# A hybrid attention and MLP layer on one core: the single heads' states and scores by token tiles of 128 instead of chunks of 64

## The chip, the cores and the metric

The program runs on one core of one Trainium2 chip. The metric is the device time of one execution in microseconds (us); less is better. Engines are named as the profile names them: PE is TensorE (PEld its weight loads), DVE is VectorE, ACT is ScalarE, POOL is GpSimd, SP is SyncE, which issues most DMAs.

## What is computed

One decoder layer over 1,024 tokens of width 1,024: an input projection, eight heads of gated linear attention (four "GLA" heads with keys 64 wide, computed two at a time as pairs, and four "HGRN2" heads with keys 128 wide, the **single heads**), an output projection and an MLP. The part that the change touches is, per head:

```
def chunk_gated_linear_attention(q, k, v, log_a, chunk):       # chunk = 64
    cum = jnp.cumsum(log_a.reshape(b, h, n, chunk, dk), axis=3)
    q_rel = q * jnp.exp(cum - cum_mid);  k_rel = k * jnp.exp(cum_mid - cum)
    scores = jnp.where(causal, jnp.einsum('bhncd,bhnsd->bhncs', q_rel, k_rel), 0.0)
    o_intra = jnp.einsum('bhncs,bhnse->bhnce', scores, v)
    k_to_end = k * jnp.exp(cum_last - cum)
    chunk_update = jnp.einsum('bhncd,bhnce->bhnde', k_to_end, v)
    # state_n+1 = exp(cum_last) * state_n + chunk_update
    o_inter = jnp.einsum('bhncd,bhnde->bhnce', q * jnp.exp(cum), states_prev)
    return o_intra + o_inter
```

## The kernel before

Everything is fp32. Large products are split into a high and a low fp32r part and made as three products over 128 rows, 128 weight columns and 512 moving columns. The products of the attention are plain fp32; each stands in the trace as **two** instructions (and two weight loads), so "x8" is four products.

The order of the work is written out by hand for every engine. The heads come in groups: P0, P1 (the paired heads), H0 (the first single head), then three times `paired` (groups 3, 4, 5: single heads 1 to 3) and `gates` (group 6). Each group projects its own head's columns and at the same time carries out the attention of the head **before** it. So the four single heads' attention lies in groups 3, 4, 5 and 6; their keys and queries are prepared in H0 (DVE function `group`) and in `paired` 3, 4 and 5.

On PE, `two_pairs` (L2051) is the order within groups 3 to 6: projection pieces P1, P2, P6, P5, P4, P3 of an early pair of column blocks, then P1, P2, P6, P5, P4, P3 of a late pair, and between them the steps of `attention_steps` (L210 to L219). With a head's two halves of 512 tokens the steps are: transposes of the keys k(0); state updates up(0); scores sc(0); k(1) and sc(1), with P4 early after them; outputs o(0); P3 early; ss(0), the sum of squares of the outputs; P1 late; up(1); P2 late; o(1); P6 and P5 late; ss(1); P4 and P3 late.

- `updates` (L1866): per half 8 (then 7) products k_nat^T v_nat, one for each chunk of 64 tokens. A chunk's rows are the lower or the upper 64 partitions, and the products alternate between them. PE waits for ACT's copies k_nat and v_nat.
- `scores` (L1853): per half four 128x128 products k_rel^T q_rel, one per tile of 128 tokens. DVE's `masks` (L2680) copies out what `causal` allows; `causal` is 0 in the block between a tile's two chunks (L946).
- `outputs` (L1884): per half four products of v_nat and the masked scores (L1893), then eight of 128 rows, 128 weight columns and 64 moving columns with the states and the queries q_cum (L1901).
- ss (L1844): ones times sq_hi and sq_lo, 512 columns each. ACT squares the outputs and makes sq_hi (L1358 to L1363); DVE makes sq_lo (`low_squares`, L2701), for which PE waits.

DVE in `paired` (L2724): states(0) (eight operations of 128 columns, each waiting for the last), masks(0), the joins of the projection's pieces, masks(1), the forget gate (L2748), low_squares(0), L2752, a scan (L2755), states(1) (seven operations), the two differences (L2759, L2762), then k_rel, k_end (L2769), a join, the copy `decay` (L2773), q_cum (L2778), q_rel (L2781), a weight sum, low_squares(1), more joins. ACT (L1402) makes the exponentials between them. POOL makes the low parts of the weights (`pair_low`, L973).

In H0 the same is done by `group` (L2455); there ACT waits for q_cum_ready (L1321) before it reads the last unit, and further down its queue come the copy k_nat (L1351) and what PE needs for up(0) of group 3.

## Time and profile before

| what | value |
|---|---|
| median of 3 runs | 1164.52 us (1164.21 to 1164.85) |
| the profiled execution, its own time | 1163.81 us |
| its span in the profile | 1162.1 us |
| granted TensorE clock, mean | 0.995 |
| PE busy | 1135.4 us, 98% of the span |
| DVE busy | 865.3 us, 74% |
| ACT busy | 612.4 us, 53% |
| POOL busy | 494.9 us, 43% |
| matmul instructions | 5555 |

The busy time of an engine counts matmuls whose ends are modelled and overlap, so 98% means that PE hardly ever stood without a matmul in flight. Groups 3 to 6 lie between some 224 and 439 us of the span.

### The profile page before, as it was taken

The numbers are of one execution on the slowest core, as the hardware profiler recorded it, in microseconds if no ns is written. First come the engines' busy times: TensorE is split into PE (matmuls) and PEld (weight loads), VectorE is DVE, ScalarE is ACT, GpSimd is POOL, SyncE is SP. The second block draws the span as 40 slices with busy tenths as digits, with TensorE's granted clock in tenths as the row PEclk, the third lists the DMA queues.
The fourth block names the chain that finished last, engine by engine and source line by source line (L and its number), as shares of the span: only waits on it lengthen the run. The fifth ranks groups of instructions, "written<-read, shape, count | busy, mean of one in ns | idle before, by whom it ended". The sixth has DMA issues, their size and how long they took to land.

```text
span 1162.1 us, 15677 instructions
## 1 busy us (share of the span) xinstructions
PE 1135.4 (98%) x5555; PEld 939.4 (81%) x5555; DVE 865.3 (74%) x1044; ACT 612.4 (53%) x933; POOL 494.9 (43%) x320
## 2 busy tenths in 40 slices
PE   7999999989999999999999999999999999999996
PEld 7788788777878788888888888888888888788886
DVE  6898887587778677377976775677795884966876
ACT  7763555756566566255654555455664433524424
POOL 1021122134243345336534343344566675665751
PEclk9999999999999999999999999999999999999999
DMA  9777387344353546722445344544624637447203
GB/s 356 263 234 272 129 202 209 79 127 134 92 173 100 155 122 213 241 77 82 143 156 184 142 156 125 182 145 159 195 64 161 220 92 264 150 133 278 71 1 145
DMA packets 162949, 186.73 MB, mean 161 GB/s; under 512 B 7604, under 2 KB 119352, under 8 KB 159928
## 3 DMA queue, kind: packets, MB, share of 16 engines
q1 hardware_dynamic: 160472, 179.44, 46.7%
q0 software_dynamic: 2400, 6.29, 2.8%
q8 instruction: 45, 0.74, 0.3%
q14 instruction: 32, 0.26, 0.1%
HBM read 138.51 MB, written 40.89 MB: 154 GB/s over the span
## 4 chain that ended last, share of the span: by engine, by line
PE 92%; DVE 2%; DMA 2%; ACT 2%; SPq 1%; issue 1%; DVEq 0%; ACTq 0%
PE unit_bank L1764 19%; PE unit_bank L2178 9%; PE unit_bank L2180 9%; PE unit_bank L2179 9%; PE small_bank L2178 9%; PE small_bank L2180 9%; PE small_bank L2179 9%; PE small_bank L1764 4%; PE unit_bank L2025 3%; PE unit_bank L2027 3%; PE unit_bank L2026 3%; PE small_bank L1901 2%; DMA ada_slot<-in_w_ada_dram 2%; PE small_bank L1803 1%; PE small_bank L1893 1%
## 5 line engine op out<-in xcount | busy, mean ns | idle before, releaser
L1016 POOL TENSOR_TENSOR wr_lo<-quarter,wr_hi 128x512 fp32r<-128x512 f32 x122 | 197.2, 1628 | 174.6 <-ACT wr_hi L1552 174.4
L2178 PE MATMUL unit_bank<-op_hi,wr_hi 128*128 128x512 f32 x452 | 176.8, 391 | 0.9 <-issue 0.9
L2180 PE MATMUL unit_bank<-op_hi,wr_lo 128*128 128x512 f32 x452 | 176.0, 389 | 0.0
L2179 PE MATMUL unit_bank<-op_lo,wr_hi 128*128 128x512 f32 x452 | 176.0, 389 | 0.0
L2178 PE MATMUL small_bank<-op_hi,wr_hi 128*128 128x512 f32 x448 | 174.6, 390 | 0.0
L2179 PE MATMUL small_bank<-op_lo,wr_hi 128*128 128x512 f32 x448 | 174.4, 389 | 0.0
L2180 PE MATMUL small_bank<-op_hi,wr_lo 128*128 128x512 f32 x448 | 174.4, 389 | 0.0
L1552 ACT ACTIVATE wr_hi<-wr_full 128x512 fp32r<-128x512 f32 x90 | 56.8, 631 | 174.8 <-DVE wr_full L2921 174.8
L2921 DVE TENSOR_TENSOR wr_full<-quarter,quarter 128x512 f32<-128x512 f32 x90 | 89.1, 991 | 56.8 <-PE small_bank L2180 22.9
L1552 ACT ACTIVATE wr_hi<-quarter 128x512 fp32r<-128x512 f32 x136 | 82.9, 626 | 89.3 <-PE unit_bank L2180 49.1
L1764 PE MATMUL unit_bank<-a_hi,w_hi 128*128 128x512 f32 x304 | 121.1, 398 | 0.0
L1764 PE MATMUL unit_bank<-a_lo,w_hi 128*128 128x512 f32 x304 | 118.5, 390 | 0.0
L1764 PE MATMUL unit_bank<-a_hi,w_lo 128*128 128x512 f32 x304 | 118.5, 390 | 0.0
L1016 POOL TENSOR_TENSOR wr_lo<-wr_full,wr_hi 128x512 fp32r<-128x512 f32 x48 | 80.5, 1680 | 77.4 <-ACT wr_hi L1552 48.1
L2178 PEld LDWEIGHTS unit_bank<-op_hi,wr_hi 128*128 128x128 f32 x452 | 84.8, 188 | 19.3 <-issue 2.1
L2180 PEld LDWEIGHTS unit_bank<-op_hi,wr_lo 128*128 128x128 f32 x452 | 84.9, 188 | 17.8
L2179 PEld LDWEIGHTS unit_bank<-op_lo,wr_hi 128*128 128x128 f32 x452 | 84.9, 188 | 17.8 <-issue 0.2
L2180 PEld LDWEIGHTS small_bank<-op_hi,wr_lo 128*128 128x128 f32 x448 | 84.1, 188 | 17.6
L2178 PEld LDWEIGHTS small_bank<-op_hi,wr_hi 128*128 128x128 f32 x448 | 84.2, 188 | 17.4 <-POOL wr_lo L1016 0.2
L2179 PEld LDWEIGHTS small_bank<-op_lo,wr_hi 128*128 128x128 f32 x448 | 84.1, 188 | 17.3
L931 POOL TENSOR_TENSOR w_lo<-raw,w_hi 128x1024 fp32r<-128x1024 f32 x11 | 29.4, 2677 | 123.9 <-ACT w_hi L1073 123.9
L973 POOL TENSOR_TENSOR pw_lo<-pw_full,pw_hi 128x512 fp32r<-128x512 f32 x24 | 36.6, 1527 | 84.2 <-ACT pw_hi L1337 69.3
(370 smaller groups left out, 2382.5 us busy)
## 6 DMA issues: line engine op xcount, KB each, us to landing
quarter<-in_w_mlp_dram SPq DMA_DIRECT2D x128, 256.0 KB, 4.1
hidden_scratch<-hid SPq DMA_DIRECT2D x98, 256.0 KB, 2.3
ada_slot<-in_w_ada_dram SPq DMA_DIRECT2D x48, 512.0 KB, 6.6
op_full<-hidden_scratch SPq DMA_DIRECT2D x21, 1024.0 KB, 4.8
pair_quarter<-in_w_in_dram SPq DMA_DIRECT2D x32, 256.0 KB, 3.6
piece_x<-t_scratch SPq DMA_DIRECT2D x16, 512.0 KB, 4.1
piece_y<-t_scratch SPq DMA_DIRECT2D x32, 256.0 KB, 3.4
raw<-in_w_out_dram SPq DMA_DIRECT2D x16, 512.0 KB, 3.9
```

The lines of the kernel that those rows point to most:

```text
L931: pool.tensor_tensor(w_lo[slot][:, :, :], raw[slot][:, :, :], w_hi[slot][:, :, :].bitcast(F32), ALU.subtract).then_inc(wlo_ready, 1)
L973: pool.tensor_tensor(pw_lo[place][:, :, :], pair_source(prod), pw_hi[place][:, :, :].bitcast(F32), ALU.subtract).then_inc(pair_lo, 1)
L1016: pool.tensor_tensor(wr_lo[slot][:, :, :], split_source(n), wr_hi[slot][:, :, :].bitcast(F32), ALU.subtract).then_inc(wr_lo_pool, 1)
L1552: act.activation(wr_hi[slot][:, :, :], split_source(n), ACT.Copy).then_inc(wr_hi_ready, 1)
L1764: return pe.matmul(out_ap, left, right, start=start, stop=stop)
L2025: pe.matmul(dst, wh, hi[:, k, :], start=k == 0 and prod not in (P6, P3), stop=False, skip_group_check=True)
L2026: pe.matmul(dst, wh, lo[:, k, :], start=False, stop=False, skip_group_check=True)
L2027: mm = pe.matmul(dst, wl, hi[:, k, :], start=False, stop=k == KH - 1, skip_group_check=True)
L2178: pe.matmul(dst, wh, ah, start=opens, stop=False, skip_group_check=True)
L2179: pe.matmul(dst, wh, al, start=False, stop=False, skip_group_check=True)
L2180: mm = pe.matmul(dst, wl, ah, start=False, stop=k == KH - 1, skip_group_check=True)
L2921: dve.tensor_tensor(dst[:, :, :], a[:, :, :], b[:, :, :], op).then_inc(w_sum, 1)
```

## The change

For the single heads the states are carried by tiles of 128 tokens. Eight states per head remain of sixteen; `updates` makes 4 (then 3) products per half over all 128 rows; `outputs` makes 3 (then 4) products of 128 moving columns with the states. For this the keys of a tile's first chunk are scaled by the decay of the second (`far_keys`), the queries of the second chunk by the decay of the first (`tile_queries`), and a tile's decay is the product of both. What a tile's second chunk takes from its first no longer goes through a state: `scores` makes, after each tile's product, one more with 128 rows, 64 weight columns (k_near, the keys of the first chunk) and 64 moving columns (q_near, the queries of the second), into the block of the scores that the mask left out, and DVE sets `causal` to 1 there (in H0). k_near and q_near are two new tiles of 128x512. PE's key transposes wait for far_keys (`k_far_ready`), the scores also for q_cum_ready. In `paired` the multiplication of k_end becomes one into k_near for the first chunks and one in place for the second; in H0 k_near is a copy. The update of the second half uses bank 3 alone. The paired heads' work is as before. The diff, cut to its core (the renamed counts of semaphores and the changed signature of update_chunks are left out):

```diff
@@ -209,12 +209,12 @@
         s[0] += [("k", 0, 0, 0)]
-        s[1] += [("up", 0, 0, 2), ("up", 1, 0, 3)]
+        s[1] += [("up", 0, 0, 2)]
         s[2] += [("sc", 0, 0, 1)]
...
         s[5] += [("ss", 0, 0, 1)]
-        s[6] += [("up", 2, 1, 3), ("up", 3, 1, 0)]
+        s[6] += [("up", 1, 1, 3)]
         s[7] += [("o", 0, 1, 2)]
@@ -248,18 +248,21 @@
     if kind == "up":
-        return (0, 0, 8)[gi] if isinstance(gi, int) and gi < 3 else 16 + 4 * (gi - 3)
+        return (0, 0, 8)[gi] if isinstance(gi, int) and gi < 3 else 16 + 2 * (gi - 3)
     if kind == "chunks":
-        return (0, 0, 30)[gi] if isinstance(gi, int) and gi < 3 else 60 + 15 * (gi - 3)
+        return (0, 0, 30)[gi] if isinstance(gi, int) and gi < 3 else 60 + 7 * (gi - 3)
     return (0, 0, 4)[gi] if isinstance(gi, int) and gi < 3 else 8 + 2 * (gi - 3)
-def update_chunks(prev, q):
-
-
-    per = 2 if prev == "P" else 4
-    first = 2 * per * (q // 2) + q % 2
-    return [n for n in range(first, first + 2 * per, 2) if n < NC - 1]
+def update_chunks(q):
+
+    first = 4 * (q // 2) + q % 2
+    return [n for n in range(first, first + 4, 2) if n < NC - 1]
+
+
+def update_tiles(half):
+
+    return [n for n in range(4 * half, 4 * half + 4) if n < TT - 1]
@@ -384,6 +383,8 @@
         decay = at("decay", 206.6875, [P, NC])
+        decay_tile = at("decay_tile", 206.65625, [P, TT])
+        k_near, q_near = at("k_near", 188.5, [P, TT, CH]), at("q_near", 190.5, [P, TT, CH])
         x_stat = at("x_stat", 206.6875, [P, TT])
@@ -1377,7 +1387,7 @@
                     if p % 2 and p < PAIRS - 1:
-                        act.wait_ge(filled["up"], before("up", FIRST_PAIRED + p // 2) + 4)
+                        act.wait_ge(filled["up"], before("up", FIRST_PAIRED + p // 2) + 2)
                     act.wait_ge(six_done, six_of(p, P1))
@@ -1832,7 +1842,10 @@
                 elif kind == "k":
-                    pe.wait_ge(k_end_ready, gi)
+                    if gi >= FIRST_PAIRED:
+                        pe.wait_ge(k_far_ready, gi - 1)
+                    else:
+                        pe.wait_ge(k_end_ready, gi)
                     mm = turn([k_end[:, t * P:(t + 1) * P] for t in range(4 * half, 4 * half + 4)], b)
@@ -1855,36 +1868,45 @@
                 pe.wait_ge(q_rel_ready, gi)
+                if prev == "H":
+                    pe.wait_ge(q_cum_ready, gi)
+                    pe.wait_ge(k_far_ready, gi - 1)
                 for i in range(4):
...
                         mm = product(SB[b][:, i * P:(i + 1) * P], k_rel[mine, t], q_rel[mine, t])
+                        if prev == "H":
+                            mm = product(SB[b][0:CH, i * P + CH:(i + 1) * P], k_near[:, 4 * half + i, :], q_near[:, 4 * half + i, :])
                         if i == 3:
...
-                width = 2 if prev == "P" else 1
                 for _, _, half, _, _ in pieces:
...
                     pe.wait_ge(read["v"], before("v", gi) + (half + 1 if prev == "P" else 0))
-                chunks = [update_chunks(prev, which) for _, which, _, _, _ in pieces]
+                if prev == "H":
+                    for _, _, half, b, _ in pieces:
+                        for n in update_tiles(half):
+                            mm = product(SB[b][:, n % 4 * P:(n % 4 + 1) * P], k_nat[:, n % 4, :], v_nat[:, 0, n, :])
+                        mm.then_inc(filled["up"], 1)
+                    return
+                chunks = [update_chunks(which) for _, which, _, _, _ in pieces]
                 for place in range(len(chunks[0])):
...
                             r = slice(CH * (n % 2), CH * (n % 2) + CH)
-                            dst = SB[b][:, place * P * width:(place + 1) * P * width]
-                            mm = product(dst, k_nat[r, (n // 2) % 4, :], v_nat[r, 0:width, n // 2, :])
+                            dst = SB[b][:, place * P * 2:(place + 1) * P * 2]
+                            mm = product(dst, k_nat[r, (n // 2) % 4, :], v_nat[r, 0:2, n // 2, :])
                             if place == len(mine) - 1:
...
-                width = 2 if prev == "P" else 1
                 for _, which, half, b, _ in pieces:
@@ -1892,8 +1914,17 @@
                                   masked[:, slot, i * P:(i + 1) * P], start=i == 0, stop=False, skip_group_check=True)
-                pe.wait_ge(read["up"], before("chunks", gi) + (8 * pieces[0][2] + 7) * width)
+                half = pieces[0][2]
+                pe.wait_ge(read["up"], before("chunks", gi) + ((8 * half + 7) * 2 if prev == "P" else 4 * half + 3))
                 pe.wait_ge(q_cum_ready, gi)
+                if prev == "H":
+                    b = pieces[0][3]
+                    for n in range(max(4 * half, 1), 4 * half + 4):
+                        mm = pe.matmul(SB[b][:, n % 4 * P:(n % 4 + 1) * P], state[:, n, :],
+                                       q_cum_of(gi - 1)[:, n * P:(n + 1) * P],
+                                       start=False, stop=n % 4 == 3, skip_group_check=True)
+                    mm.then_inc(filled["o"], 1)
+                    return
                 for c in range(8):
@@ -1989,7 +2020,7 @@
                     both.append(p)
-                    if len(both) == (2 if prev == "P" or p[0] == "up" else 1):
+                    if len(both) == (2 if prev == "P" else 1):
                         {"sc": scores, "up": updates, "o": outputs}[p[0]](prev, both, gi)
@@ -2452,6 +2483,23 @@
+            def far_keys():
+
+                dve.tensor_tensor(chunk_of_tiles(k_end, 0), k_near[:, :, :], decay_of(1).broadcast_to([P, TT, CH]), ALU.mult
+                                  ).then_inc(k_far_ready, 1)
+
+            def tile_queries(dst, q, since, gi):
+
+                dve.wait_ge(decay_ready, gi + 1)
+                then(dve.tensor_tensor(decay_tile[:, :].rearrange("p (n i) -> p n i", i=1), decay_of(0), decay_of(1), ALU.mult), False)
+                then(dve.scalar_tensor_tensor(q_near[:, :, :], chunk_of_tiles(q, 1), 0.5, chunk_of_tiles(since, 1),
+                                              ALU.mult, ALU.mult), False)
+                dve.scalar_tensor_tensor(chunk_of_tiles(dst, 0), chunk_of_tiles(q, 0), 0.5, chunk_of_tiles(since, 0),
+                                         ALU.mult, ALU.mult)
+                dve.wait_ge(setup, chain[0])
+                dve.tensor_tensor(chunk_of_tiles(dst, 1), q_near[:, :, :], decay_of(0).broadcast_to([P, TT, CH]), ALU.mult
+                                  ).then_inc(q_cum_ready, 1)
+
@@ -2577,6 +2625,9 @@
                 read_out(4)
+                if own == "H":
+                    dve.wait_ge(read["sc"], before("sc", FIRST_PAIRED))
+                    then(dve.memset(causal[0:CH, CH:P], 1.0), False)
                 if prev == "P":
@@ -2599,17 +2650,22 @@
                 if prev:
-                    dve.wait_ge(read["up"], before("chunks", gi) + (30 if prev == "P" else 15))
+                    dve.wait_ge(read["up"], before("chunks", gi + 1))
                 dve.wait_ge(e_cum, gi + 1)
...
                 finished("o")
-                dve.scalar_tensor_tensor(q_cum[:, :], t0[:, :], factor, cum[:, :], ALU.mult, ALU.mult
-                                         ).then_inc(q_cum_ready, 1)
+                if own == "H":
+                    tile_queries(q_cum, t0, cum, gi)
+                else:
+                    dve.scalar_tensor_tensor(q_cum[:, :], t0[:, :], factor, cum[:, :], ALU.mult, ALU.mult
+                                             ).then_inc(q_cum_ready, 1)
                 if name == "P1":
...
                     weight_sum_of(0, "S2")
+                    then(dve.tensor_copy(k_near[:, :, :], chunk_of_tiles(k_end, 0)))
+                    far_keys()
                 read_out(7)
@@ -2688,14 +2744,13 @@
                     done = before("chunks", gi)
-                    dve.wait_ge(filled["up"], before("up", gi) + at_["up", 2 * half + 1][1] + 1)
-                    for n in range(8 * half, min(8 * half + 8, NC - 1)):
-                        which = 2 * half + n % 2
-                        place = update_chunks("H", which).index(n)
+                    b, place = at_["up", half]
+                    dve.wait_ge(filled["up"], before("up", gi) + place + 1)
+                    for n in update_tiles(half):
                         if n:
                             dve.wait_ge(read["up"], done + n)
-                        dve.scalar_tensor_tensor(state[:, n + 1, :], state[:, n, :], decay[:, n:n + 1],
-                                                 SB[at_["up", which][0]][:, place * P:(place + 1) * P], ALU.mult, ALU.add
+                        dve.scalar_tensor_tensor(state[:, n + 1, :], state[:, n, :], decay_tile[:, n:n + 1],
+                                                 SB[b][:, n % 4 * P:(n % 4 + 1) * P], ALU.mult, ALU.add
                                                  ).then_inc(read["up"], 1)
@@ -2766,16 +2821,21 @@
                 dve.wait_ge(e_end, gi + 1)
-                dve.tensor_tensor(k_end[:, :], k_end[:, :], t1[:, :], ALU.mult).then_inc(k_end_ready, 1)
+                dve.wait_ge(filled["sc"], before("sc", gi + 1))
+                then(dve.tensor_tensor(k_near[:, :, :], chunk_of_tiles(k_end, 0), chunk_of_tiles(t1, 0), ALU.mult), False)
+                dve.tensor_tensor(chunk_of_tiles(k_end, 1), chunk_of_tiles(k_end, 1), chunk_of_tiles(t1, 1), ALU.mult
+                                  ).then_inc(k_end_ready, 1)
                 join(late, "11")
...
                 dve.wait_ge(decay_ready, gi + 1)
+                dve.wait_ge(setup, chain[0])
+                far_keys()
                 dve.wait_ge(c_read["11"], C_READ_0["11"] + early + 1)
                 dve.wait_ge(c_read["12"], C_READ_0["12"] + early + 1)
-                dve.scalar_tensor_tensor(own_cum[:, :], q_rel[:, :], 0.5, own_cum[:, :], ALU.mult, ALU.mult).then_inc(q_cum_ready, 1)
+                tile_queries(own_cum, q_rel, own_cum, gi)
                 dve.wait_ge(e_q, gi + 1)
```

## Rows read from the trace of the kernel before

**Rows 1.** The page: busy time of PE, and the chain that ended last.
```profile
PE 1135.4 (98%) x5555; PEld 939.4 (81%) x5555; DVE 865.3 (74%) x1044; ACT 612.4 (53%) x933; POOL 494.9 (43%) x320
...
PE 92%; DVE 2%; DMA 2%; ACT 2%; SPq 1%; issue 1%; DVEq 0%; ACTq 0%
```

**Rows 2.** Waits of PE, whole span: us in total, times, longest.
```profile
PE small_bank L1764 <- DVE sq_lo L2704: 3.8, 6, 1.0
PE small_bank L1764 <- ACT k_nat L1351: 3.5, 1, 3.5
```

**Rows 3.** Timeline of PE, groups 3 and 4: start, us, line, tile, count, idle before.
```profile
241.83 1.05 PE L1764 MATMUL small_bank<-q_rel,k_rel 128*128 128x128 f32 x8
242.63 0.48 PE L2025 MATMUL unit_bank<-t_hi,pw_hi 128*128 128x512 f32 x1
...
250.23 1.05 PE L1893 MATMUL small_bank<-masked,v_nat 128*128 128x128 f32 x8
251.12 1.90 PE L1901 MATMUL small_bank<-q_cum,state 128*128 128x64 f32 x16
252.83 0.48 PE L2025 MATMUL unit_bank<-a_hi,pw_hi 128*128 128x512 f32 x1
...
259.08 0.39 PE L2026 MATMUL unit_bank<-a_lo,pw_hi 128*128 128x512 f32 x1
259.30 0.39 PE L2027 MATMUL unit_bank<-a_hi,pw_lo 128*128 128x512 f32 x1
259.62 1.16 PE L1764 MATMUL small_bank<-v_nat,k_nat 64*128 64x128 f32 x14
260.71 0.50 PE L2025 MATMUL unit_bank<-a_hi,pw_hi 128*128 128x512 f32 x1
...
290.44 1.16 PE L1764 MATMUL small_bank<-v_nat,k_nat 64*128 64x128 f32 x16
291.53 0.50 PE L2025 MATMUL unit_bank<-a_hi,pw_hi 128*128 128x512 f32 x1
```

**Rows 4.** Timeline of PE's weight loads, group 3: scores, then updates.
```profile
241.60 1.08 PEld L1764 LDWEIGHTS small_bank<-q_rel,k_rel 128*128 128x128 f32 x8
...
259.62 0.96 PEld L1764 LDWEIGHTS small_bank<-v_nat,k_nat 64*128 64x128 f32 x14 [0.35 <-issue]
```

**Rows 5.** Timeline of DVE, group 4.
```profile
305.66 1.83 DVE L2748 TENSOR_SCALAR t<-t,misc 128x1024 f32<-128x1024 f32 x1
307.94 1.26 DVE L2704 TENSOR_TENSOR sq_lo<-stat,sq_hi 128x512 fp32r<-128x512 f32 x1 [0.44 <-ACT sq_hi L1363]
...
314.01 2.65 DVE L2697 SCALAR_TENSOR_TENSOR state<-state,decay,small_bank 128x128 f32<-128x128 f32 x7
316.58 1.22 DVE L2759 TENSOR_TENSOR t<-q_cum 128x1024 f32<-128x1024 f32 x1
...
327.81 0.69 DVE L2704 TENSOR_TENSOR sq_lo<-stat,sq_hi 128x512 fp32r<-128x512 f32 x1
```

**Rows 6.** Timelines of ACT and of POOL, group 4.
```profile
306.30 0.60 ACT L1360 ACTIVATE stat<-small_bank 128x512 f32<-128x512 f32 x1 [0.74 <-PE small_bank L1901]
...
305.66 1.28 POOL L973 TENSOR_TENSOR pw_lo<-pw_full,pw_hi 128x512 fp32r<-128x512 f32 x1 [3.36 <-DVE pair_quarter L2625]
306.90 1.74 POOL L973 TENSOR_TENSOR pw_lo<-pair_quarter,pw_hi 128x512 fp32r<-128x512 f32 x1
```

**Rows 7.** Timelines of DVE, ACT and PE from H0 into group 3.
```profile
222.54 1.21 DVE L2607 SCALAR_TENSOR_TENSOR q_cum<-t,cum 128x1024 f32<-128x1024 f32 x1
...
223.79 0.60 ACT L1209 ACTIVATE t<-unit_bank 128x512 f32<-128x512 f32 x1
...
234.93 2.08 PE L1764 MATMUL small_bank<-v_nat,k_nat 64*128 64x128 f32 x16 [3.46 <-ACT k_nat L1351]
```

**Rows 8.** Timelines of DVE and PE, group 6: sq_lo(0) and ss(0).
```profile
414.32 0.68 DVE L2704 TENSOR_TENSOR sq_lo<-stat,sq_hi 128x512 fp32r<-128x512 f32 x1
...
415.15 0.47 PE L1764 MATMUL small_bank<-sq_hi,ones 128*128 128x512 f32 x1
```

## Prediction before the run

> **What bounds the kernel now.** I read the page first: PE is busy 98% of the span and carries 92% of the chain that ended last [rows 1]. So a microsecond less on PE is worth up to one, unless PE then stands before a wait. Next the waits of PE: two kinds fall in the part that is changed [rows 2]. One is the wait of ss for DVE's sq_lo, six times, 3.8 us, twice in each of groups 3 to 5. The other is 3.5 us before up(0) of group 3. They matter more than their size, for they show where DVE and ACT and not PE set the time: what PE saves just before such a wait comes back as a longer wait. Then the timelines: of PE for the price of each small product [rows 3], of its weight loads [rows 4], of DVE, ACT and POOL for the chain into the two sq_lo [rows 5, 6], of the passage from H0 to group 3 [rows 7], and of group 6 [rows 8].
>
> **PE, per head: what goes.** An fp32 product is two instructions.
> - Updates: half 0 takes 1.09 us for 8 products (290.44 to 291.53), half 1 1.09 for 7 (259.62 to 260.71). Before a group of them PE loses another 0.1: the product of 512 columns ahead takes 0.32 (259.30 to 259.62) where the one before it takes 0.22 [rows 3]. Products over all 128 rows are priced by the scores: 0.80 for 4, 0.20 each [rows 3]. Half 0: 1.09 + 0.1 - 0.80 = 0.4 less. Half 1, with 3 products: 1.19 - 0.60 = 0.6 less.
> - Outputs with the states: 8 products of 64 columns take 1.71 (251.12 to 252.83). The 4 of 128 columns on v_nat take 0.89. So half 0 with 3 saves 1.71 - 0.67 = 1.04, half 1 with 4 saves 0.82 [rows 3].
> - Together 2.86 us per head.
>
> **PE, per head: what comes.** Eight products with 64 weight columns and 64 moving columns, each between products with 128 weight columns. No row has 64 weight columns. The nearest change of shape is that of the updates, 64 rows among 128. There the first weight load is not made ahead: for the scores it starts 0.23 before its product, for the updates at the same time as its product, after 0.35 of idleness [rows 4]. In the rows the new shape starts 0.07 before the end of the product ahead: 259.30 + 0.39 = 259.69 against 259.62, and on the way back 259.62 + 1.16 = 260.78 against 260.71 [rows 3]. With no change of shape the next starts 0.25 before that end (241.83 + 1.05 = 242.88 against 242.63). One small product lasts 1.05 - 7 x 0.11 = 0.27 [rows 3]. So, if the 64-column shape changes as the 64-row shape does: from the last instruction of a tile's product 0.20 to the small one, 0.06 to 0.10 to its second instruction, 0.15 to 0.20 back, together 0.41 to 0.50 in place of 0.10. That is 0.31 to 0.40 for each, 2.5 to 3.2 us for eight; I take 2.9, in the upper part, since the first load after a change is late as well. The other bound, with no cost for the change of shape: 0.20 each like the scores, or 0.12 if a load of half the columns takes about half, 0.96 to 1.6 for eight. I take the first because it is the only change of shape in the trace, and it costs on both sides.
>
> The Trainium skill, TensorEngine Tiling (Array Packing), Key Properties and Available Configurations, counts 128x64 as a tiling mode of its own and says that changing the mode drains TensorE. By that rule the sum keeps the 2.9; without it, it takes the 0.96 to 1.6. For the change to 64 rows the trace agrees; for 64 columns no row shows it.
>
> **What lies beside DVE's chain.** From the end of P4 early on, DVE works without a pause to sq_lo(0) and on to sq_lo(1), so PE's savings in o(0), up(1) and o(1), 1.04 + 0.6 + 0.82 = 2.46, are lost in the waits at ss(0) and ss(1) unless the chain itself gets shorter. Does it?
> - sq_lo(0): it waited 0.44 for ACT, and ACT waited 0.74 for o(0) [rows 5, 6]. It then lasted 1.26 where 0.69 is its time elsewhere (at 327.81) [rows 5]: it ended 0.56 after POOL's operation that ran from 306.90 to 308.64 [rows 6]. POOL had slipped in while DVE waited for ACT. L2748 likewise lasted 1.83 and ended 0.55 after POOL's first [rows 5, 6]. With o(0) 1.04 shorter, ACT is ready 0.74 earlier, DVE need not wait, and sq_lo(0) follows L2748 directly: ready at about 308.1 and not 309.2. Gain 1.0 (0 if POOL gets in all the same). Reading it so: DVE and POOL take turns at something, and who asks first holds it.
> - States(1): 7 operations in 2.57, 0.37 each [rows 5]; 4 fewer: -1.47.
> - Added on DVE before sq_lo(1): far_keys, one operation over 512 columns, 0.6 (0.69 less the overlap of 0.09). For q_cum, three over 512 and the small decay_tile in place of one over 1024: 1.8 + 0.1 - 1.13 = +0.77. k_end in two pieces +0.07. Waits on its own results some 0.2. Sum +1.64. Less the 1.47: +0.2.
> - The chain from P4 to ss(1) changes by -1.0 + 0.2 = **-0.8** in groups 3, 4, 5. What is late next is still sq_lo(1): PE's wait there grows from at most 1.0 [rows 2] to about 2.5.
>
> **From ss(1) to the next P4** PE waits for nothing in groups 3 to 5, so its own work counts in full: -0.4 + 2.9.
>
> **H0.** q_cum_ready lets ACT go on at 223.79, and from there ACT works in a row to k_nat, for which PE stood idle for 3.46 [rows 7]. tile_queries takes 0.77 more than the one operation, with its waits 0.9. It lies on the path: **+0.9**. The memset, k_near's copy and far_keys there end before or about when PE comes to the key transposes, which have the wait of 3.46 behind them to hide in: nothing, or 0.6 to 1.3 if that cover were gone. In `paired`, k_far_ready and q_cum_ready come half a group before PE asks: nothing.
>
> **Group 6** makes no keys or queries. Its sq_lo(0) ends at 415.00 at the end of an unbroken row of DVE's work from P4, and ss(0) starts at 415.15 with no idle time [rows 8]: the 1.04 of o(0) is lost there. sq_lo(1) is ready early, so up(0), up(1) and o(1) count: -0.4 - 0.6 - 0.82 + 2.9 = **+1.1**. After it PE is the bound, and DMA traffic is unchanged.
>
> **Sum.** Groups 3 to 5: 3 x (-0.4 - 0.8 + 2.9) = +5.1. H0 +0.9, group 6 +1.1: +7.1. The profiled execution took 1163.8 (span 1162.1), so 1170.9; the median of the runs lies 0.7 above it: **1171.6 us**. A measurement of this kernel can tell about 0.2%, 2.3 us, from no change.
>
> **Rivals.**
> 1. *The new shape costs nothing extra.* Eight products 0.96 to 1.6. Groups 3 to 5: 3 x (-0.24 to +0.4); H0 +0.9; group 6 -0.9 to -0.2. Sum -0.7 to +1.9: 1163.8 to 1166.4, no change. For it: within their group the 64-row products follow each other every 0.07 to 0.08 per instruction [rows 3]. Against: both edges of such a group cost time.
> 2. *Faster.* DVE's chain moves with PE, so that all of the 2.86 counts: for this low_squares(1) would have to come 1.6 us sooner still, that is DVE would have to have been held up by PE and not by its own row of work. With small products at 0.12 to 0.20 each: 4 x (-1.90 to -1.26) + 0.9 = -6.7 to -4.1, 1157.8 to 1160.4. It decides if a small product costs under 0.26 and the waits at ss don't grow. Against: PE waits for sq_lo in each of those groups already [rows 2].
> 3. *Slower still.* The same as my forecast, but POOL gets in before sq_lo(0) all the same, and the small products cost 0.40: +3.0 and +1.2, 1175.8.
> That the change doesn't do what it says I can exclude but for a few per cent: the counts of products follow from the loops.
>
> **How the numbers follow.** The forecast with its upper neighbour (1168 to 1176) has 0.58, no change 0.28, faster 0.12, the rest 0.02. Faster by over 0.2% is below 1162.2: 0.12. Within 0.2% (to 1166.8): 0.26. Slower: 0.62. The range leaves out the faster case and reaches from the lower edge of the second case, 1163.8, to 1176.0; the likeliest case's own range is 1168 to 1176.
>
> **What would show it.** In the profile after: scores of a half, 8 instructions of 128 columns mixed with 8 of 64, taking over 2.0 us from their start to P5 or P4 (0.80 before); under 1.4 speaks for rival 1. PE's wait for sq_lo(1) at 2 us or more in groups 3 to 5; if it stays under 1.2, rival 2 holds. sq_lo(0) back at 0.7 us with no wait for ACT. The wait for k_nat in group 3 at 4.3. Scores under 1.4 with a time above 1168 would mean that DVE's chain grew, by far_keys or by turns with POOL, and that my -0.8 is wrong.

## The result and the profile after

The changed kernel takes **1179.38 us** (median of 4 runs, 1178.21 to 1180.89) against 1164.68 before on the same chip: ratio 1.0122, 95% interval 1.0110 to 1.0135. It is slower by 14.7 us. I had forecast 1171.6 (+7.1) and a range from 1163.8 to 1176.0: the direction was right, the size was not. The profiled execution took 1178.21, its span is 1176.5 (before 1162.1).

The page and the waits of PE, after, where [rows 1, 2] stood before:

```profile
PE 1141.0 (97%) x5483; PEld 941.0 (80%) x5483; DVE 859.1 (73%) x1033; ACT 612.4 (52%) x933; POOL 493.9 (42%) x320
...
PE 88%; DVE 5%; issue 3%; ACT 1%; DMA 1%; SPq 1%; DVEq 0%; ACTq 0%
```

```profile
PE small_bank L1774 <- DVE sq_lo L2759: 12.3, 7, 3.6
...
PE small_bank L1774 <- issue: 4.1, 1, 4.1
```

PE has fewer instructions (5483 for 5555), and yet takes longer: the wait for sq_lo grew from 3.8 us to 12.3, the one for k_nat in group 3 from 3.5 to 4.1 (the releaser is now put down as "issue").

**PE's timeline, group 3.** The scores of half 0, then o(0), up(1); it answers to [rows 3]:

```profile
241.90 0.38 PE L1774 MATMUL small_bank<-q_rel,k_rel 128*128 128x128 f32 x2
242.21 0.33 PE L1774 MATMUL small_bank<-q_near,k_near 128*64 128x64 f32 x2
242.47 0.49 PE L1774 MATMUL small_bank<-q_rel,k_rel 128*128 128x128 f32 x2
242.89 0.33 PE L1774 MATMUL small_bank<-q_near,k_near 128*64 128x64 f32 x2
...
244.50 0.50 PE L2056 MATMUL unit_bank<-t_hi,pw_hi 128*128 128x512 f32 x1
...
253.96 1.05 PE L1915 MATMUL small_bank<-masked,v_nat 128*128 128x128 f32 x8
254.84 0.83 PE L1923 MATMUL small_bank<-q_cum,state 128*128 128x128 f32 x6
...
261.93 0.83 PE L1774 MATMUL small_bank<-v_nat,k_nat 128*128 128x128 f32 x6
```

Scores of a half took 0.80 and now take 244.50 - 241.90 = 2.60: 0.45 for each product of 64 columns. State products and updates are about as cheap as priced: three state products take 0.59 to the next instruction (254.84 to 255.43), three updates 0.58 (261.93 to 262.51), where 0.67 and 0.60 were priced.

**Where a group grew.** DVE's join 21 marks the end of P4 early; from it DVE's chain runs to ss(1), and from ss(1) PE runs to the next P4. First the kernel before (PE, DVE), then after:

```profile
275.57 0.47 PE L1764 MATMUL small_bank<-sq_hi,ones 128*128 128x512 f32 x1 [0.96 <-DVE sq_lo L2704]
284.53 1.06 PE L1803 MATMUL small_bank<-ident,vT 128*128 128x128 f32 x8
...
328.64 0.47 PE L1764 MATMUL small_bank<-sq_hi,ones 128*128 128x512 f32 x1 [0.92 <-DVE sq_lo L2704]
```

```profile
303.68 0.70 DVE L2664 TENSOR_TENSOR unit_bank<-unit_bank,k_end 128x512 f32<-128x512 f32 x1 [0.82 <-PE unit_bank L2027]
```

```profile
279.06 0.47 PE L1774 MATMUL small_bank<-sq_hi,ones 128*128 128x512 f32 x1 [3.57 <-DVE sq_lo L2759]
...
280.36 0.63 PE L2058 MATMUL unit_bank<-t_hi,pw_lo 128*128 128x512 f32 x1
280.79 0.63 PE L2056 MATMUL unit_bank<-t_hi,pw_hi 128*128 128x512 f32 x1
...
282.92 0.49 PE L2058 MATMUL unit_bank<-t_hi,pw_lo 128*128 128x512 f32 x1
283.24 0.40 PE L2056 MATMUL unit_bank<-t_hi,pw_hi 128*128 128x512 f32 x1
...
289.38 1.03 PE L1813 MATMUL small_bank<-ident,vT 128*128 128x128 f32 x8
...
336.54 0.47 PE L1774 MATMUL small_bank<-sq_hi,ones 128*128 128x512 f32 x1 [3.56 <-DVE sq_lo L2759]
```

- ss(1) of group 3 to join 21 of group 4: 28.11 before, 32.58 after: **+4.47**.
- join 21 to ss(1) of group 4: 24.96 before, 24.90 after: **-0.06**.

The first part holds a term that I had not seen. Behind the wait of 3.57 us, products of the same size follow each other every 0.43 us and not every 0.23, and ss(1) to the v transposes takes 10.32 where it took 8.96. The granted clock says why (windows of the changed kernel; after the duration come PE, PEld, DVE, ACT, POOL busy, then PEclk):

```profile
275.00:279.00 4.00, 0.49 (x3) 0.06 (x1) 3.90 (x7) 0.59 (x2) 0.00 (x0) 1.00 0.59 193
279.00:283.00 4.00, 3.94 (x11) 3.13 (x12) 3.09 (x5) 2.29 (x5) 2.37 (x2) 0.59 0.85 240
283.00:287.00 4.00, 4.00 (x19) 3.33 (x18) 2.02 (x4) 3.96 (x6) 0.43 (x2) 0.99 0.06 25
```

PE stood idle for most of the first window and got 0.59 of its clock in the second, that is mostly the lower level, 1.2 GHz. So 4.47 is -0.4 for up(0), + 2 x 1.80 for the scores, + 1.36 for the clock (10.32 - 8.96), within 0.1.

**DVE and POOL, group 4**, for the chain; they answer to [rows 5, 6]. First two of DVE's and one of POOL's in the kernel before, then DVE and POOL after:

```profile
309.12 0.68 DVE L2752 TENSOR_SCALAR t<-t 128x1024 f32<-128x1024 f32 x1
...
323.69 2.27 DVE L2778 SCALAR_TENSOR_TENSOR q_cum<-q_rel,q_cum 128x1024 f32<-128x1024 f32 x1
```

```profile
323.58 1.29 POOL L973 TENSOR_TENSOR pw_lo<-pair_quarter,pw_hi 128x512 fp32r<-128x512 f32 x1
```

```profile
311.64 0.70 DVE L2720 TENSOR_TENSOR unit_bank<-unit_bank,k_end 128x512 f32<-128x512 f32 x1 [3.29 <-PE unit_bank L2058]
...
313.47 0.81 DVE L2803 TENSOR_SCALAR t<-t,misc 128x1024 f32<-128x1024 f32 x1
314.83 1.14 DVE L2759 TENSOR_TENSOR sq_lo<-stat,sq_hi 128x512 fp32r<-128x512 f32 x1 [0.56 <-ACT sq_hi L1373]
315.90 1.77 DVE L2807 TENSOR_SCALAR t<-t 128x1024 f32<-128x1024 f32 x1
...
327.68 1.78 DVE L2825 TENSOR_TENSOR k_near<-k_end,t 128x512 f32<-128x512 f32 x1
...
335.71 0.69 DVE L2759 TENSOR_TENSOR sq_lo<-stat,sq_hi 128x512 fp32r<-128x512 f32 x1
```

```profile
313.62 1.80 POOL L983 TENSOR_TENSOR pw_lo<-pw_full,pw_hi 128x512 fp32r<-128x512 f32 x1 [6.61 <-DVE pair_quarter L2681]
315.39 1.74 POOL L983 TENSOR_TENSOR pw_lo<-pair_quarter,pw_hi 128x512 fp32r<-128x512 f32 x1
...
327.05 1.87 POOL L983 TENSOR_TENSOR pw_lo<-pw_full,pw_hi 128x512 fp32r<-128x512 f32 x1 [3.90 <-ACT pw_hi L1347]
```

sq_lo(0) ends 4.33 us behind the start of join 21, where it ended 5.52 behind it before. But then t1 (L2807) lasts 1.77, which took 0.68 before, and k_near 1.78, where an undisturbed operation on 128x512 takes 0.69: each runs beside a split on POOL. The kernel before has such operations as well, and one of them I had overlooked: q_cum (L2778) lasts 2.27 beside POOL's split from 323.58, where the same operation in H0 takes 1.21 [rows 7]; it does so in groups 3, 4 and 5 alike. What DVE loses beside splits in the chain of group 4 is 2.6 us before (1.02 in L2748, 0.57 in sq_lo(0), 1.05 in q_cum) and 2.6 after (0.45 in sq_lo(0), 1.09 in t1, 1.09 in k_near): it has moved, not shrunk. By stretches, the -0.06 of the chain is (us, after less before)

```
to the end of sq_lo(0)                 -1.19      k_rel's end to the join (k_near, k_end)   +1.18
from there to states(1)                +1.11      far_keys and the queries                  +0.29
states(1), 3 operations for 7          -1.55      all else                                  +0.10
```

**Passage to group 3 and group 6** (PE; [rows 7, 8]):

```profile
235.19 1.93 PE L1774 MATMUL small_bank<-v_nat,k_nat 128*128 128x128 f32 x8 [4.13 <-issue]
...
430.84 0.47 PE L1774 MATMUL small_bank<-sq_hi,ones 128*128 128x512 f32 x1 [1.01 <-DVE sq_lo L2759]
```

The span's 14.4 us, by stretches: up to up(0) of group 3 +0.26 (this run was already 0.5 early ahead of the first changed operation on the path: DVE's copy `decay` in H0 starts at 221.92 and not at 222.46); from there to ss(1) +3.23; the periods from ss(1) to ss(1) of groups 4 and 5 +4.41 and +4.47; from ss(1) of group 5 to ss(0) of group 6 +3.3; from there to the end -1.3 (up(1) and o(1), shorter).

### The profile page after: what moved, and what is told of

Same layout as the page of the kernel before. It is cut to its first block, busy times and chain, and to the rows that moved or that the text cites. A ratio compares the mean times of both kernels' runs of the same rounds, so it can differ in the third digit from the quotient of the medians.

```text
span 1176.5 us, 15521 instructions
## 1 busy us (share of the span) xinstructions
PE 1141.0 (97%) x5483; PEld 941.0 (80%) x5483; DVE 859.1 (73%) x1033; ACT 612.4 (52%) x933; POOL 493.9 (42%) x320
## 4 chain that ended last, share of the span: by engine, by line
PE 88%; DVE 5%; issue 3%; ACT 1%; DMA 1%; SPq 1%; DVEq 0%; ACTq 0%
PE unit_bank L1774 19%; PE unit_bank L2209 9%; PE unit_bank L2211 9%; PE unit_bank L2210 9%; PE small_bank L2209 9%; PE small_bank L2210 9%; PE small_bank L2211 9%; PE small_bank L1774 4%; PE unit_bank L2056 3%; PE unit_bank L2057 2%; PE unit_bank L2058 2%; PE small_bank L1813 1%; DVE ada_acc L2310 1%; DMA ada_slot<-in_w_ada_dram 1%; PE small_bank L1915 1%
## 5 line engine op out<-in xcount | busy, mean ns | idle before, releaser
L983 POOL TENSOR_TENSOR pw_lo<-pair_quarter,pw_hi 128x512 fp32r<-128x512 f32 x32 | 48.4, 1514 | 64.3 <-ACT pw_hi L1347 64.3
```

Of the source, the lines that this page charges most:

```text
L983: pool.tensor_tensor(pw_lo[place][:, :, :], pair_source(prod), pw_hi[place][:, :, :].bitcast(F32), ALU.subtract).then_inc(pair_lo, 1)
```

## Experiments

Times are medians; a ratio is against the kernel before on the same chip, with its interval. The runs were made on several chips (the kernel before at 1164.5 to 1165.3), so differences of medians between runs hold to about 1 us.

**The near products: left out, grouped, widened.**

```
e1:  -  mm = product(SB[b][0:CH, ...], k_near[:, 4 * half + i, :], q_near[:, 4 * half + i, :])
     -  then(dve.memset(causal[0:CH, CH:P], 1.0), False)
e2:  the four near products moved behind the loop over the four of 128 columns
e3:  +  at_ = min(4 * half + i, TT - 2)
     +  mm = product(SB[b][:, ...], flat(k_near[:, at_:at_ + 2, :]), q_near[:, 4 * half + i, :])
```

> The kernel after without the 32 products of 64 weight columns and without the memset that opens the mask: what a tile's second chunk takes from its first is left out. Theory (the change of shape costs PE 0.45 us for each, in full): scores of a half back at 0.80 us, 14.4 us less than after, so about 1165, although PE then does less than before; PE's wait at ss(1) stays at 3.5 us and the clock falls after it. Rival (the products matter little, DVE's longer work is the cost): under 5 us less, above 1174.

> The same work as after, but in each half first the four products of 128 weight columns, then the four of 64, so that the shape changes twice and not eight times. Theory (it is the changes that cost): a half's scores take about 1.55 us (0.80 + 4 x 0.12 + 0.25) in place of 2.60, 8.4 us less than after, about 1171. Rival (the small product itself costs 0.45): no difference, 1179.

> The changed kernel, but the near product of a tile (the block of scores between its two chunks) takes 128 weight columns (the near keys of two tiles) instead of 64, and so writes all 128 rows beside the tile's diagonal block: the order of the 16 products, their rows to stream and their reads stay, only the shape of the weights is now the same in all. The scores of the second chunk against itself are overwritten, which changes that part of the result. Theory (a product whose shape differs from its neighbours' costs 0.45 us instead of about 0.23, half of it for the change of shape): the scores of a half take about 1.6 to 1.7 us instead of 2.60, near the grouped form, each of four heads gains 1.8 to 2.0 us, and the time is 1171 to 1173. Rival (four more products cost it, whatever their shape; what grouping saved came from elsewhere): 2.4 us or more for a half, 1177 to 1180.

Measured: e1 1165.32, 1.0006 [0.9996, 1.0016]; e2 1172.46, 1.0069 [1.0054, 1.0084]; e3 1174.60, 1.0084 [1.0070, 1.0097]. PE in e2, then in e3:

```profile
243.73 1.05 PE L1774 MATMUL small_bank<-q_rel,k_rel 128*128 128x128 f32 x8
244.71 0.68 PE L1774 MATMUL small_bank<-q_near,k_near 128*64 128x64 f32 x8
245.32 0.50 PE L2059 MATMUL unit_bank<-t_hi,pw_hi 128*128 128x512 f32 x1
```

```profile
244.00 0.33 PE L1774 MATMUL small_bank<-q_near,k_near 128*128 128x64 f32 x2
244.17 0.44 PE L1774 MATMUL small_bank<-q_rel,k_rel 128*128 128x128 f32 x2
244.45 0.33 PE L1774 MATMUL small_bank<-q_near,k_near 128*128 128x64 f32 x2
```

Scores of a half: 2.60 alternating, 1.59 grouped, 1.71 alternating with 128 columns (243.78 to 245.49). The order of e3 is that of the change, and it moves twice the weights; only the shape is the same throughout. So a near product costs 0.45 us in the change and 0.23 with the shape of its neighbours: 0.22 of it is there only because the shapes differ. The rows of e2 part it another way. Its four small products follow each other every 0.15 (244.71 to 245.32), and the four large ones ahead of them take 0.98 where 0.80 is usual, 0.18 for the one change and back. Set against 0.15 the alternating order pays 0.30 for each. By the Trainium skill, TensorEngine Tiling (Array Packing), Key Properties, a change of the tiling mode drains TensorE: the trace agrees, with 0.18 to 0.30 us for a change and back. The forecast of e1 held, but for its wait at ss(1), 2.5 and not 3.5; e2 gained 6.9 us, not 8.4. e3 saved 0.9 per half and yet only 4.8 us in all, against 6 to 8 forecast; the clock tells why (below).

**The lower clock.** A fill of useless products keeps PE going ahead of the wait at ss(1), groups 3 to 5: on the change (e5), on the grouped form (e12), and without near products (e15, leaves that block out).

```
+  if u0 is None and half == 1 and gi < 6:
+      for _ in range(14):
+          product(SB[b][:, :], ones_r[:, :], tok(a_hi[:, 0], 0))
   pe.wait_ge(sq_lo_ready, before("split", gi) + at_n + 1)
```

> After, with 14 additional products of 128x512 on PE (3.2 us of work without use, into the bank that ss(1) overwrites) just ahead of its wait for sq_lo in groups 3 to 5. Theory (the idleness lowers the clock, and that costs 1.3 us each time): the wait shrinks to 0.4, the products after ss(1) follow each other every 0.23 us and not every 0.43, 3 x 1.3 = 4 us less than after in spite of more work, about 1175. Rival (the slow stretch comes from something else): no difference or slower, 1179 to 1180.

> The changed kernel with the four products of 64 columns after the four of 128, and with 14 products whose result nobody reads ahead of the wait at ss(1) in groups 3 to 5, so that TensorE does not stand still there. Each edit alone gave -6.9 us and -3.3 us. If the price of the shape and the lower clock behind the 3.6 us of idleness are two terms of one sum: 1168 to 1170. Rival (they overlap, for instance because the grouped products are what ran at the lower clock): 1171 to 1173.

> The changed kernel without its near products (the block of scores between a tile's two chunks is left out, and with it that part of the result) and with the 14 products that nobody reads ahead of the wait at ss(1). Theory (three separate terms: the products, their change of shape, the lower clock behind the wait): the run without near products gave 1165.3 and still had the lower clock behind 2.5 us of idleness; without it 1160.5 to 1162.5, so that the four token-tiled heads as such are 2 to 4 us faster than the kernel before, and the eight near products cost 1.3 to 1.6 us per head grouped and 3.3 to 3.6 alternating. Rival (the clock's price stands only behind the longer wait): 1164.5 to 1166, as without the fill.

Measured: e5 1176.11, 1.0099 [1.0084, 1.0114]; e12 1167.03, 1.0016 [1.0007, 1.0025]; e15 1162.18, 0.9976 [0.9967, 0.9985]. PE in e5:

```profile
277.01 3.33 PE L1774 MATMUL small_bank<-a_hi,ones 128*128 128x512 f32 x14
280.66 0.50 PE L1774 MATMUL small_bank<-sq_hi,ones 128*128 128x512 f32 x1 [0.31 <-DVE sq_lo L2762]
...
289.67 1.06 PE L1813 MATMUL small_bank<-ident,vT 128*128 128x128 f32 x8
```

ss(1) to the v transposes is 9.01 again, as before the change (8.96). In the profiled executions the three stretches took (us, groups 3, 4, 5):

```
before      8.96  8.92  9.01      after, filled (e5)     9.01  9.21  9.02
after      10.32 10.31  9.08      without near (e1)     10.31 10.32  8.91
grouped e2 10.33 10.06 11.41      wide near (e3)        11.46 10.34 11.51
t1 first e9 10.34 10.37  8.89
```

PE's waits ahead of these stretches are 0.96 us at most before, 2.5 in e1, 3.3 to 3.6 after, in e2 and in e3, and 1.8 in e9 (below; there ss(0) waited 1.9 as well). Behind the 0.96 the clock stayed (1.00 from 276 to 285 in the kernel before); behind the others it mostly fell, not every time and not equally. Above 8.96 this is 2.8 us in the change, 4.9 in e2, 6.4 in e3. It closes the accounts about: e5 gained 3.3, e12 5.4 over e2 (3.3 were expected), and my estimate, a median less the price in one execution, puts e3 without it at 1168.2, e2 at 1167.6. What is left between 1162.18 and 1167.03, 4.9 us, are the grouped near products, 1.2 us per head; alternating they cost 13.9 us (1176.11 - 1162.18), 3.5 per head. And the token tiles without near products, e15, beat the kernel before by 2.8 us, although their fill ends 0.7 us behind sq_lo(1) in each group. It leaves out a part of the result, so it says what the tiles alone are worth and not what a whole kernel takes.

**VectorE's chain.** Is it its length, its place or its last link that is late? low_squares(1) ahead of the tile's queries (e4); with the sum for P3 too, far_keys later (e6); t1 ahead of low_squares(0) (e9).

```
e4:  low_squares(1)                                          ahead of tile_queries(own_cum, ...)
e6:  weight_sum_of(late, "S4"); low_squares(1)               ahead of it; far_keys() behind weight_sum_of(late + 1, "S3")
e9:  low_squares(0)                                          behind the tensor_scalar that makes t1
```

> After, with DVE's sq_lo of the second half moved ahead of the queries' operations in groups 3 to 5; the same work. Theory (DVE's chain sets ss(1), and TensorE's lower clock after the 3.5 us of idleness is an effect of it): the wait at ss(1) falls from 3.5 to under 0.4, no stretch at about 0.6 of the clock behind it, 3 x (3.2 + 1.3) = 13 us less than after, about 1166. Rival 1 (the wait goes but turns up at the next thing that DVE delivers later): under 5 us less. Rival 2 (the clock falls for another reason): 9.6 us less, 1170.

> The changed kernel with VectorE's queue reordered in the paired groups alone: the weight sum for P3 of the late pair and low_squares(1) go ahead of the tile's queries, and far_keys goes behind the next pair's first weight sum, where VectorE idles 1.3 us for GpSimd. Moving low_squares(1) alone gave nothing, since TensorE then waited 2.4 us at P3 for the split of that sum and 1.6 us for vT. Theory (the tail of VectorE's queue behind the states is what carries 3.6 us of wait and 1.3 us of a lower TensorE clock per group): no wait at ss(1), none at P3, clock 1.00 behind it, some 1.3 us of wait for vT before the v transposes remain (ScalarE's chain of log, exp and two splits starts about 2.9 us behind that sum's quarter); a group of 57.5 us falls to about 54, and the time is 1167 to 1170. Rival (the late thing is ScalarE's or GpSimd's own queue, as the run before hinted): the waits for vT grow to 3 us or more, a group stays above 56, the time is 1175 or more.

> The changed kernel; in the paired groups low_squares(0), which waits 0.56 us for ScalarE, goes behind the operation on t1 (L2807) instead of ahead of it. It bears on the step of the prediction that priced VectorE's chain from P4 to ss(1) at -0.8: measured, that chain takes 24.90 us (311.64 to 336.54), where it was 24.96 before (303.68 to 328.64), although sq_lo(0) did come about 1.2 earlier against it, because t1 then lasted 1.77 instead of 0.68 beside GpSimd's split. Theory (the gap at sq_lo(0) lets GpSimd's next split in, and the operation behind it pays): with no wait ahead of t1 the chain is 1.0 to 1.6 shorter, the wait at ss(1) 2.0 to 2.6 instead of 3.57, the time 1175 to 1177. Rival (GpSimd's two splits overlap whatever runs there, so a turn is only handed on): the chain stays at 24.9 within 0.3, and the time is 1178.5 to 1180.

Measured: e4 1179.76 (1.0131 [1.0115, 1.0146]), e6 1175.61 (1.0089 [1.0072, 1.0107]), e9 1179.27 (1.0128 [1.0113, 1.0143]). Three misses of my theory; in e4 and e9 a rival came out as told, in e6 the time did, but for another wait than its rival named. Waits of PE in e4, in e6:

```profile
PE unit_bank L2056 <- POOL pw_lo L983: 6.9, 3, 2.4
PE small_bank L1813 <- ACT vT L1410: 4.9, 3, 1.7
```

```profile
PE unit_bank L2056 <- DVE unit_bank L2720: 6.8, 3, 2.3
```

With sq_lo(1) early, PE waits at P3 for the split of the sum that DVE makes behind the queries; with that sum early too, for the join 22. So it is not one operation that is late, but everything behind the row of DVE's work. DVE in e9:

```profile
315.38 1.67 DVE L2806 TENSOR_SCALAR t<-t 128x1024 f32<-128x1024 f32 x1
316.97 1.75 DVE L2759 TENSOR_TENSOR sq_lo<-stat,sq_hi 128x512 fp32r<-128x512 f32 x1
...
331.24 1.73 DVE L2488 TENSOR_TENSOR k_end<-k_near,decay 128x512 f32<-128x512 f32 x1
```

Without a pause ahead of t1, POOL's splits still cost three operations about 1 us each, now t1, sq_lo(0) and far_keys; the chain is 24.83 us (312.71 to 337.54). PE's wait only parted: 1.9 at ss(0) and 1.8 at ss(1), 12.0 us in all as against 12.3. The Trainium skill, SBUF — State Buffer, "SBUF: two separate sides", has a GpSimd operation and certain VectorE ones (with two inputs in SBUF, or in a two-port mode) exclude each other at a shared pair of ports: whichever starts first holds it for the whole instruction. The trace agrees: k_near, from 327.68, ends 0.54 us behind the split that ran from 327.05 to 328.92, and 0.69 is all that it takes undisturbed. The cost goes to whatever stands there, so that what I counted as won at sq_lo(0) was handed on.

**Orders of the queues, with the kernel before as control.** Can the token tiles win with their queues written for them? e7 is e6 with grouped products. e10 also moves the joins u and 22 ahead of the queries and ScalarE's value_of(1), log and exp ahead of the tanh; e13 puts ScalarE's value copies and high parts and then the tanh ahead of log and exp, and join 21 and the next sum ahead of the silu, join 12 ahead of the norms; e16 puts that tanh ahead of the high parts. e8, e11, e14 and e17 are the same orders in the kernel before (without far_keys, which it does not have; e17 with u and 22 behind the queries).

```
e16, DVE:  S4(late) low_squares(1) join u, 22 | tile_queries q_rel | join 21, S3(next) silu gate far_keys S2(next) join 12
e16, ACT:  value_of(1) tanh(11) | pair_high(P1) value_of(0) pair_high(P7) pair_high(P2) | norm_log(1) norm_exp(1)
```

> The reordered queue of VectorE (as in the run with the weight sum and low_squares(1) ahead, far_keys behind) together with the four products of 64 columns after the four of 128 instead of between them. Grouping alone gave -6.9 us against the changed kernel. If costs on TensorE and the wait at ss(1) add up, as two lengths of one path: 1160 to 1164, so the token tiles would be level with the kernel before or slightly faster. Rival (VectorE and ScalarE's chain now sets the group, so that shorter TensorE work only makes their waits longer): 1165 to 1169, near the reordered run without grouping.

> The kernel before (states by chunks of 64), with the same move in VectorE's queue: the weight sum for P3 of the late pair and low_squares(1) ahead of the queries' two products. It says what of the reordered runs belongs to the order and what to the token tiles. The kernel before waits 2.8 us in all at ss(1) in three groups, and its v transposes start 0.14 us behind the end of vT. Theory: the three waits of about 0.96 us go, half of it comes back at vT: 1162 to 1164. Rival (a group of the kernel before is held by TensorE's own 52 us and by vT alike): no change, 1164 to 1165.

> Grouped products, and VectorE's and ScalarE's queues in the paired groups written for this kernel: VectorE does the weight sum for P3, low_squares(1) and the joins u and 22 of the late pair ahead of the tile's queries, far_keys behind the next pair's first sum; ScalarE does value_of(1), log and exp of the norm ahead of the tanh that waits for q_rel. In the run with only the sum and low_squares(1) moved, TensorE waited 2.3 us per group for the join 22 at the end of q_rel. Theory (nothing but the order of VectorE's tail holds the groups, and TensorE's own work per group is 1.3 us less than before's): no wait over 1.2 us in groups 3 to 5 and clock 1.00, a group of 51 to 52.5 us, the time 1157 to 1163, under the kernel before. Rival (ScalarE's chain to vT takes over): waits of 2 to 3 us for vT, 1164 to 1168.

> The kernel before with the same order of VectorE's and ScalarE's queues, as the control of the run beside it. With the sum and low_squares(1) alone moved, it gained nothing, since it then waited three times, 2.7 us in all, for vT; ScalarE's log and exp now come ahead of the tanh that waits for q_rel, so that these waits should go too. Theory: what is left to gain are the 2.8 us of its waits at ss(1): 1161.5 to 1163.5. Rival (another wait takes their place): 1164 to 1166.

> Grouped products and a second order of the queues. In the run before (1172.97) TensorE waited 2.7 us per group for GpSimd's split of the next pair's first weights, since ScalarE made their high part only behind log and exp. Now ScalarE makes value_of(1), that high part, value_of(0), the next two high parts and the tanh first, then log and exp of the norm; VectorE does the sum for P3, low_squares(1), joins u and 22, the queries, join 21, the next pair's first sum, silu, gate, far_keys, the second sum, join 12. Theory (only the order of the tail holds the groups): waits under 1 us each, clock 1.00, 1158 to 1163, under the kernel before. Rival (VectorE's added operations leave no order without a late one): a new wait of over 1.5 us per group, 1165 or more.

> The kernel before with the second order of the queues, the control of the run beside it. Theory: with VectorE's shorter tail nothing is late but GpSimd's splits; its 2.8 us at ss(1) go: 1161.5 to 1163.5. Rival: as with the first order, another wait of about 2.5 us per group, 1169 to 1176.

> As the run e13_tuned (grouped products, VectorE's order), but ScalarE makes the tanh of the late pair ahead of the high part of the next pair's first weights: there that high part waited 2.6 us for its transfer, the tanh, which stood behind it, came at 282.25, and TensorE waited 2.7 to 3.6 us for the silu that frees its bank. Here the tanh can start at 279.9, the silu at about 281, and the split for GpSimd ends at about 282.4 where TensorE arrives at 281.0. Theory (the order alone holds the group): a wait of 1.0 to 1.6 us there, clock 1.00, a group of 52 to 53, the time 1158 to 1162, under the kernel before. Rival (each order has its late one): another wait of over 2 us per group, 1165 to 1171.

> The kernel before with the same order on ScalarE, and on VectorE the sum for P3 and low_squares(1) ahead of the queries, the joins u, 22, 21 behind them. It is the control: the sum and low_squares(1) alone moved gave 1166.1, with 2.7 us of waits for vT, and value_of(0) no longer stands behind log and exp here. Theory: 1161.5 to 1164. Rival: the join 22 or the silu of the late pair becomes late, 1166 or more.

```
                       token tiles, grouped              kernel before
sum, sq_lo(1) early    e7  1166.82 [1.0010, 1.0027]      e8  1166.05 [1.0001, 1.0019]
second                 e10 1172.97 [1.0056, 1.0084]      e11 1175.25 [1.0078, 1.0105]
third                  e13 1170.63 [1.0035, 1.0060]      e14 1173.36 [1.0053, 1.0080]
fourth                 e16 1166.60 [1.0005, 1.0023]      e17 1166.82 [1.0009, 1.0026]
```

The intervals are those of the ratio to the kernel before. All eight missed their theory; e8, e10 and e11 are above the range of their rival too. Every order has its late one. Waits of PE in e10, in e13, in e16:

```profile
PE unit_bank L2059 <- POOL pw_lo L983: 8.1, 3, 2.7
```

```profile
PE unit_bank L2059 <- DVE t L2729: 9.0, 3, 3.6
```

```profile
PE unit_bank L2079 <- issue: 5.0, 3, 1.7
...
PE unit_bank L2059 <- POOL pw_lo L983: 4.3, 3, 1.4
```

With an order of its own and grouped products the change is 0.05 to 0.23% behind the kernel before, 12.8 us better than as it was made, and no version with the whole result beats the kernel before. Grouped products and the fill, with the queues as they were (e12, 1167.03), come as near; fill and order together were not run. In the second and third order the tiles are 2.3 and 2.7 us faster than the chunks. In the first (0.8 slower) and the fourth (0.2 faster) the difference is smaller than the spread of the runs of one kernel, over 2 us, so that none is shown. Whether an order without a late operation exists stays open; the wait of 1.7 at the next pair's last piece (L2079, in the kernel before L2045) was not followed up.

## Why the prediction was right and wrong

- **PE's savings, 2.86 per head: right.** Three products over 128 rows take 0.58 to 0.59 to the next instruction in up(1) and in o(0), where 0.60 and 0.67 were priced. The run without near products (e1) is level with the kernel before because its waits took the saving back: 4 x 2.86 = 11.4 saved, but 13.1 us of waits for sq_lo instead of 3.8, 2.7 of lower clock and the 0.8 of H0.
- **A near product at 0.36: mis-sized, 0.45.** The step gave two instructions and the way there and back 0.41 to 0.50 "in place of 0.10". The pitch in the rows after is 0.31 to 0.42 from the 128-column pair to the small one and 0.26 back, and the load after each change of shape is not ahead of its product. The reason was right (e2, e3), the sum short by 0.7 us per head, **2.8** in all. Rival 1 (no cost of the shape) is refuted by e2 and e3.
- **"The chain from P4 to ss(1) changes by -0.8": failed, -0.06.** The step that failed is "with o(0) 1.04 shorter ... sq_lo(0) follows L2748 directly ... Gain 1.0". sq_lo(0) came 1.2 earlier against the join, and the next operation, t1 beside POOL's split, paid 1.1 of it back. The other terms came out near their sum, but not by my reading: I took q_cum in the kernel before at 1.13, where it lasted 2.27 beside a split. So far_keys and the queries added 0.29 and not 1.57, while k_end in two pieces, with k_near now beside a split, added 1.18 and not 0.07. That these two cancel is luck. Three such losses, 2.6 us per chain, are there before, after and, with 3.1, in e9; the prediction counted on one of them to go. I had granted this case only a place in rival 3. Three groups: **2.2**.
- **What the wait at ss(1) does to the clock: missing.** I let the wait grow to 2.5 and costed it at what it lost; it grew to 3.57 (3.4 of it are the 0.96 and the 2.46 that PE saved beside the chain, with the chain no shorter), and PE came out of it at the lower clock: **2.8** in this execution (e5: 3.3). The trace before showed it: after the wait of 3.46 [rows 7] the updates of half 0 last 2.08, where those of group 4 take 1.16 [rows 3].
- **H0: right**, +0.76 against +0.9, once the 0.5 of the unchanged start is set right. **Group 6**: +2.0 against +1.1, 0.7 of it the near products' size.
- Sum: 7.1 + 2.8 + 2.2 + 2.8 = 14.9. The medians differ by 14.7; the terms were read from the profiled executions, whose spans differ by 14.4, with the early start of 0.5 in them. Of the signs looked for, the scores over 2.0, the wait over 2 and the wait for k_nat (4.13 for 4.3) were there; sq_lo(0) at 0.7 without a wait for ACT was not: it took 1.14 behind a wait of 0.56.
- **Rival 2**, faster, was refuted as argued: the chain kept its length with PE's work beside it 2.46 shorter, and e4 and e6 show that DVE's row of work, not PE, holds the stretch.

## What to carry to other kernels

Where an engine that is saved on then waits, ask what that wait costs behind it: here a third of the loss unforeseen was PE's clock after a 3.6 us pause, which no sum of instructions shows. Keep products of one shape together, or pay for the wider shape: 0.22 us for a product whose shape differs from its neighbours' is as much as a product of 128 columns costs (0.20). And price the added operations of the chain engine at their full length even where each fits somewhere: when the queue is a row without gaps, moving the one that is waited for only hands the wait to the next. Read the operations that run beside another engine's for their real length: one here lasted 2.27 and was counted as 1.13.

## What the runs showed that I had not expected

- The clock's price for the same wait of 3.6 us varies from 0.1 to 2.5 us, within one execution (e2) from 1.1 to 2.5.
- Fewer weight columns can cost more: the near product took 0.45 with 64 and 0.23 with 128, in the same order. Among its own kind the one with 64 is the cheaper, 0.15.
- k_near, 128x512, took 0.69 in e9, and POOL's split beside it 3.08 instead of 1.28: there the split waited, 1.8 us, through several of DVE's operations, where a split costs DVE about 1.05.
